# Both feed-forward products by seven quadrant products per 1024 block, inner rows and merged rows through DRAM

## The reference, cut to what matters

```python
D_MODEL, SEQ, D_FF = 1024, 1024, 4096
...
y = g[:, :, 0] * y_a + g[:, :, 1] * y_b + g[:, :, 2] * y_c
mix = y @ w_out
x = x + rmsnorm(mix, ln_mix_post)
h = rmsnorm(x, ln_mlp_pre)
x = x + rmsnorm(jnp.square(jax.nn.relu(h @ w_up)) @ w_down, ln_mlp_post)
```

## Time and profile before

| | before |
|---|---|
| median of 3 runs | 4586.25 us (4578.94 to 4586.79) |
| the profiled execution: its own time, its span | 4588.66 us, 4586.9 us |
| mean granted TensorE clock | 0.965 |
| busy share of the span: PE, DVE, ACT, POOL | 91%, 55%, 39%, 14% |
| last section (`closing`) | merge stage from about 3735 us, matmuls of the feed-forward part 3873.0 to 4576.3 us, end at 4586.9 us |

### The profile page before, as it was taken

One profiled execution on the slowest core, in us unless ns is written; L12 is line 12 of the kernel. 1 busy time (PEld: TensorE's weight loads), 2 busy tenths in 40 slices (PEclk: granted clock), 3 DMA queues, 4 the chain that ended last, 5 costly groups with the idle time before them and its releaser, 6 DMA issues. The chain is left out here.

```text
span 4586.9 us, 66646 instructions
## 1 busy us (share of the span) xinstructions
PE 4186.2 (91%) x26765; PEld 3263.0 (71%) x26765; DVE 2513.5 (55%) x3323; ACT 1799.9 (39%) x3273; POOL 657.2 (14%) x759
## 2 busy tenths in 40 slices
PE   7999889889988979999999997788589979999999
PEld 1887667668756767888887785565388855888887
DVE  1413777651277756555656553787577756334333
ACT  0312456431145642222223333777566513423222
POOL 0200400020030010000102200776212101000000
PEclk9999999999999989999999998899799989999999
DMA  7434411134331131333333232112211056323322
GB/s 268 160 112 155 143 60 49 63 135 142 117 128 55 44 129 56 119 102 103 117 101 120 101 120 78 47 62 89 95 43 39 30 200 236 110 101 129 101 92 83
DMA packets 250802, 485.61 MB, mean 106 GB/s; under 512 B 33048, under 2 KB 73208, under 8 KB 250124
## 3 DMA queue, kind: packets, MB, share of 16 engines
q1 hardware_dynamic: 250512, 481.60, 30.4%
HBM read 360.42 MB, written 121.13 MB: 105 GB/s over the span
## 5 line engine op out<-in xcount | busy, mean ns | idle before, releaser
L1028 DVE TENSOR_TENSOR p_tl<-spare,p_th 128x1024 fp32r<-128x1024 f32 x156 | 199.4, 1279 | 359.4 <-ACT p_th L900 359.4
L900 ACT CAST p_th<-spare 128x1024 fp32r<-128x1024 f32 x156 | 163.5, 1049 | 566.7 <-PE p_ps L852 566.7
L316 PE MATMUL p_ps<-p_wh,hi 128*128 128x512 f32 x896 | 352.2, 393 | 5.7 <-DVE p_wl L484 5.7
L316 PE MATMUL p_ps<-p_wh,lo 128*128 128x512 f32 x896 | 350.2, 391 | 0.0
L316 PE MATMUL p_ps<-p_wl,hi 128*128 128x512 f32 x896 | 350.1, 391 | 0.0
L852 PE MATMUL p_ps<-p_th,p_xh 128*128 128x512 f32 x784 | 310.2, 396 | 2.0 <-DVE p_tl L1028 2.0
L852 PE MATMUL p_ps<-p_th,p_xl 128*128 128x512 f32 x784 | 309.9, 395 | 0.0
L852 PE MATMUL p_ps<-p_tl,p_xh 128*128 128x512 f32 x784 | 309.9, 395 | 0.0
L852 PE MATMUL p_ps<-p_xh,p_th 128*128 128x512 f32 x672 | 263.1, 391 | 1.0 <-DVE p_tl L1028 1.0
L852 PE MATMUL p_ps<-p_xh,p_tl 128*128 128x512 f32 x672 | 263.7, 392 | 0.0
L852 PE MATMUL p_ps<-p_xl,p_th 128*128 128x512 f32 x672 | 262.6, 391 | 0.0
(11 more groups left out here) (422 smaller groups left out, 9902.8 us busy)
## 6 DMA issues: line engine op xcount, KB each, us to landing
spare<-w_in SPq DMA_DIRECT2D x56, 1024.0 KB, 5.6
p_raw<-w_in SPq DMA_DIRECT2D x40, 1024.0 KB, 5.9
pn_dram<-p_stg SPq DMA_DIRECT2D x128, 256.0 KB, 2.0
spare<-w_down SPq DMA_DIRECT2D x32, 1024.0 KB, 4.8
spare<-w_up SPq DMA_DIRECT2D x30, 1024.0 KB, 5.3
p_dram<-p_stg SPq DMA_DIRECT2D x112, 256.0 KB, 2.1
m_w<-w_mod SPq DMA_DIRECT2D x12, 2048.0 KB, 11.8
pt_dram<-p_stg SPq DMA_DIRECT2D x96, 256.0 KB, 2.2
```

The costliest lines, as they stand in the source:

```text
L316: mm = pe.matmul(ps[:, u, :], lhsT, rhs, start=(kk == 0 and q == 0), stop=(kk == KD - 1 and q == 2))
L900: act.copy(th[:, g % 2], (R11, T, R21, R12, R22, R11, R21)[i][:, 2 * u:2 * u + 2]).then_inc(s_hi, 1)
L1028: dve.tensor_tensor(tl[:, g % 2], (R11, T, R21, R12, R22, R11, R21)[i][:, 2 * u:2 * u + 2], th[:, g % 2], ALU.subtract).then_inc(s_lo, 1)
```

## The change

Both feed-forward products are now done like the projections, for all 1024 rows at once: each 1024x1024x1024 block, four for w_up and four for w_down, is seven products of 512x512x512 quadrants and sums of quadrants, 14 units of 24 matmuls (56 products of 48 matmuls, 2688 matmuls; 3072 before). A unit is still three fp32r matmuls for each tile of a pair.

- *Up block.* x, turned and normed, stands in four quadrants A11 to A22; five more of the seven operands are made of them once (S1 to S4), and all seven are split into xh and xl (128x2048 each; five of the splits stand in the queues of the first up block). The weight quadrants R11 to R22 are loaded per block, T1 to T4 are their sums on VectorE, and each unit is cast (th, ACT) and its remainder made (tl, DVE). The product tiles are joined on VectorE (`joined`), relu is on ScalarE, and the square is now on GpSimd (64 of 128x512). SP stores the result to `h_dram`.
- *Down block.* Hidden quadrants H11 to H22 come back from `h_dram`; their sums are four 128x2048 operations a block on GpSimd, in place, and both operands of every unit are split on the fly (th, tl and sh, sl). Product tiles are added into seven accumulators (`gathered`); with the last block GpSimd and VectorE combine these, ScalarE makes row sums behind waits for them (s_u2, s_c21, s_c22) that stand between its casts, and `final` adds the result to the merged rows.
- *Merge stage.* The residual rows have two buffers, xr, in place of x_sb; the merged rows go to `xm_dram` (`store_x`) and come back at the end. The load of a tile's rows waits for the store and the norm of the tile two before (s_xst, s_nx), and stands on SP ahead of the inputs of a later row tile. All eight row tiles are normed here; `turned_dram` is gone.
- *Addresses.* `sums` (160 bytes) and `ab2` stand ahead of `spare`, whose place is free in `closing`.

The diff, cut to its core:

```diff
-                    sp.wait_ge(s_y, NT)
+                if t >= 2:
+                    sp.wait_ge(s_xst[t % 2], 16 * (t // 2))
+                    sp.wait_ge(s_nx, t - 1)
+                sp.dma_start(xr[:, t % 2, :], C.x_dram[DEPTH - 1][t * P:(t + 1) * P, :]).then_inc(s_x[t % 2], 16)
+
+            def store_x(t):
+                sp.wait_ge(s_xf, t + 1)
+                sp.dma_start(xm_dram[t * P:(t + 1) * P, :], xr[:, t % 2, :]).then_inc(s_xst[t % 2], 16)
...
+                q = NQ + f
+                sp.wait_ge(s_S4, f + 1)
+                sp.wait_ge(s_hl, UN * f + 6)
+                load_hidden(f + 1, 0)
+                sp.wait_ge(s_hl, UN * f + 8)
+                load_hidden(f + 1, 3)
+                sp.wait_ge(s_lo, UN * q + 8)
+                load_block(q + 1, 2)
+                sp.wait_ge(s_hl, UN * f + 10)
+                load_hidden(f + 1, 2)
+                sp.wait_ge(s_lo, UN * q + 10)
+                load_block(q + 1, 0)
+                sp.wait_ge(s_lo, UN * q + 12)
+                load_block(q + 1, 1)
+                sp.wait_ge(s_hl, UN * f + 14)
+                load_hidden(f + 1, 1)
+                sp.wait_ge(s_lo, UN * q + 14)
+                load_block(q + 1, 3)
...
+            def triples(n, u, j, cols):
+                x = XS[n % NOPS]
+                b = (2 * n + u) % 2
...
+                    else:
+                        pairs = ((sh[:, b, k, cols], th[:, b, k, :]), (sh[:, b, k, cols], tl[:, b, k, :]), (sl[:, b, k, cols], th[:, b, k, :]))
...
+                act.copy(th[:, n % 2], source(n)).then_inc(s_hi, 1)
+                if n >= UP:
+                    v = n - UP
+                    f = v // UN
+                    ready, count = ((s_H[0], 16 * (f + 1)), (s_H[1], 16 * (f + 1)), (s_S2, f + 1), (s_H[3], 16 * (f + 1)), (s_S3, f + 1), (s_S1, f + 1), (s_S4, f + 1))[i]
+                    act.wait_ge(ready, count)
+                    act.copy(sh[:, v % 2], hidden(v)).then_inc(s_hh, 1)
...
+            for n in range(16 * NQ):
+                pool.wait_ge(s_r, n + 1)
+                x = stg[:, n % 4, :]
+                pool.tensor_tensor(x, x, x, ALU.mult).then_inc(s_q, 1)
+            for f in range(NQ):
+                pool.wait_ge(s_H[2], 16 * (f + 1))
+                pool.wait_ge(s_H[3], 16 * (f + 1))
+                if f > 0:
+                    pool.wait_ge(s_hl, UN * (f - 1) + 12)
+                else:
+                    pool.wait_ge(s_xl, 4)
+                pool.tensor_tensor(HS[:], H21[:], H22[:], ALU.add).then_inc(s_S1, 1)
+                pool.drain()
+                pool.wait_ge(s_H[0], 16 * (f + 1))
+                pool.tensor_tensor(H21[:], H11[:], H21[:], ALU.subtract).then_inc(s_S3, 1)
+                pool.drain()
+                pool.wait_ge(s_hl, UN * f + 2)
+                pool.tensor_tensor(H11[:], HS[:], H11[:], ALU.subtract).then_inc(s_S2, 1)
+                pool.drain()
+                pool.wait_ge(s_hl, UN * f + 4)
+                pool.tensor_tensor(H12[:], H12[:], H11[:], ALU.subtract).then_inc(s_S4, 1)
+            pool.wait_ge(s_C, last + 8)
+            pool.tensor_tensor(c11[:], c11[:], a1[:], ALU.add).then_inc(s_c11, 1)
+            pool.wait_ge(s_C, last + 12)
+            pool.tensor_tensor(u6[:], u6[:], a1[:], ALU.add).then_inc(s_u2, 1)
+            pool.drain()
+            pool.tensor_tensor(p3[:], p3[:], u6[:], ALU.add).then_inc(s_pre, 1)
+            pool.wait_ge(s_C, last + 16)
+            pool.tensor_tensor(p4[:], p4[:], u6[:], ALU.add).then_inc(s_pre, 1)
+            pool.wait_ge(s_fp, 16)
+            pool.wait_ge(s_sq, HT)
+            gain(c11, 0)
+            pool.wait_ge(s_C, last + 20)
+            pool.tensor_tensor(u6[:], u6[:], p7[:], ALU.add).then_inc(s_u3, 1)
+            pool.wait_ge(s_sq, 2 * HT)
+            gain(p4, 0)
...
+            def unit_lo(n):
+                if n >= ALL:
+                    return
+                dve.wait_ge(s_hi, n + 1)
+                dve.tensor_tensor(tl[:, n % 2], source(n), th[:, n % 2], ALU.subtract).then_inc(s_lo, 1)
+                if n >= UP:
+                    v = n - UP
+                    dve.wait_ge(s_hh, v + 1)
+                    dve.tensor_tensor(sl[:, v % 2], hidden(v), sh[:, v % 2], ALU.subtract).then_inc(s_hl, 1)
...
+            def T1(q):
+                for b in range(2):
+                    dve.wait_ge(s_R[b], 16 * (q + 1))
+                dve.tensor_tensor(R12, R12, R11, ALU.subtract).then_inc(s_T1, 1)
+
+            def T2(q):
+                dve.wait_ge(s_R[3], 16 * (q + 1))
+                dve.drain()
+                dve.tensor_tensor(T[:], R22, R12, ALU.subtract).then_inc(s_T2, 1)
...
+            def gathered(f, i, j):
+                n = NP + NOPS * f + i
+                dve.wait_ge(s_pm, 4 * n + j + 1)
+                to = acc[i][:, j, :]
+                if f == 0:
+                    dve.tensor_copy(to, tile(n, j)).then_inc(s_C, 1)
+                else:
+                    dve.tensor_tensor(to, to, tile(n, j), ALU.add).then_inc(s_C, 1)
...
+            def final(n, t, first, second):
+                dve.wait_ge(s_rs, n + 1)
+                j = t % HT
+                x = xrow(t)
+                dve.tensor_tensor(second[:, j, :], second[:, j, :], post[:, CH:], ALU.mult)
+                dve.scalar_tensor_tensor(x[:, 0:CH], first[:, j, :], ms[:, t, 3:4], x[:, 0:CH], ALU.mult, ALU.add)
+                dve.drain()
+                dve.scalar_tensor_tensor(x[:, CH:], second[:, j, :], ms[:, t, 3:4], x[:, CH:], ALU.mult, ALU.add).then_inc(s_fx, 1)
...
+            for n in range(ALL):
+                q, i, u = n // UN, n % UN // 2, n % 2
+                unit_lo(n + 2)
+                if n % UN == 0:
+                    T1(q)
+                elif n % UN == 1:
+                    T2(q)
+                elif n % UN == 3:
+                    T4(q)
+                elif n % UN == 5:
+                    T3(q)
...
+                    for j in range(4):
+                        gathered(f, i, j)
+                        if f == NQ - 1 and i == 6:
+                            final(j, HT + j, p4, u6)
+                    if f == NQ - 1 and i == 4:
+                        dve.wait_ge(s_pre, 2)
+                        dve.drain()
+                        for j in range(4):
+                            dve.tensor_tensor(p4[:, j, :], p4[:, j, :], p7[:, j, :], ALU.add).then_inc(s_c21, 1)
+                    if f == NQ - 1 and i == 5:
+                        dve.wait_ge(s_u3, 1)
+                        dve.drain()
+                        for j in range(4):
+                            dve.tensor_tensor(u6[:, j, :], u6[:, j, :], w5[:, j, :], ALU.add).then_inc(s_c22, 1)
+                        for j in range(4):
+                            dve.tensor_tensor(p3[:, j, :], p3[:, j, :], w5[:, j, :], ALU.add)
+                        dve.drain()
...
-        spare = sb("spare", [P, KD * D])
+        C.ab = sb("ab2", [P, NT, 2 * C_HEADS])
+        C.sums = sb("sums", [P, 8 + 4 * NT])
+        s4 = s2.enter_context(ExitStack())
+        spare = sb("spare", [P, KD * D], F32, s4)
...
```

More of the change, by code:

```diff
@@ L3208, in closing @@
         s_x = [sem(f"x_loaded{b}") for b in range(2)]
+        s_xst = [sem(f"merged_rows_stored{b}") for b in range(2)]
         s_y = sem("y_ready")
@@ L3306, in _ @@
-            for t in range(TT):
-                store(0, t)
-            for n in range(NW + 1, 2 * NW):
-                for b in range(2):
-                    weights(b, n)
-            for t in range(TT):
-                store(1, t)
+                if t == NT - 3:
+                    sp.wait_ge(s_y, NT - 1)
+                    for b in range(4):
+                        load_block(0, b)
+                if t >= 1:
+                    store_x(t - 1)
+                    if t + 1 < NT:
+                        load_x(t + 1)
@@ L3313, in _ @@
+            sp.wait_ge(s_c11, 1)
+            sp.wait_ge(s_u2, 1)
+            sp.dma_start(post, ins["ln_mlp_post_2"][0].partition_broadcast(P)).then_inc(s_fp, 16)
+            for n, t in enumerate([*range(HT, NT), *range(HT)]):
+                sp.wait_ge(s_fx, n + 1)
+                store_out(t)
             sp.wait_ge(s_out, 16 * NT)
@@ new lines, in partial, with relu @@
+            def partial(q, j):
+                act.wait_ge(s_pm, 4 * NOPS * q + j + 1)
+                if q > 0:
+                    act.wait_ge(s_C, ADDS * (q - 1) + added[5] + 2 * j + 1)
+                else:
+                    act.wait_ge(s_sum, 4)
+                act.copy(U1[:, j, :], tile(NOPS * q, j)).then_inc(s_U, 1)
+            def relu(q, i, j):
+                act.wait_ge(s_C, ADDS * q + added[i] + (2 * j if i == 5 else j) + 1)
+                act.activation(stg[:, j, :], stg[:, j, :], ACT.Relu).then_inc(s_r, 1)
@@ L3497, in _, with row_sums @@
+            def row_sums(t, half, rows):
+                act.activation(waste, rows[:, t % HT, :], ACT.Square, accum_out=ms[:, t, half:half + 1]).then_inc(s_sq, 1)
```

(51 more changed lines are left out.)

599 lines of the change are left out of this document (296 added, 303 removed).

## The result

The changed kernel takes **4627.44 us** (median of 4 runs, 4622.98 to 4632.63) against 4586.52 before, 40.9 us slower. The ratio on record is 1.0093, 95% interval 1.0075 to 1.0110 (the two medians alone give 1.0089). Forecast were 4624, a range of 4572 to 4668, and slower with a chance of 0.73.

A forecast was written before the change was run, and what follows sets the result against it. TensorE's gapless matmul stream was taken as the bound: 87.0 us saved by fewer matmuls and 5.5 of waits, against added delays, summed to +38; 4588.66 + 38 - 2.4 gave 4624 us, range 4572 to 4668.

The forecast's parts named there:

- merge stage: Stage before the feed-forward products: loads wait behind the store and norm, so y comes late; +5.5 us (0 to 14).
- before the first product: Start of the up product: last transposes wait for square, roots and scaled copy, 6.0 plus 2.0 of clock; +8 us.
- first up block; others: Up product: queued splits of x make units 6 and 8 late, +5.5 us; other up blocks +2.
- down blocks, all: Down product: +24.5 us at the first block, +36 at three boundaries, +40 in the last block.
- tail: After the last matmul: VectorE is four tiles behind, 15.4 us where 6.4 passed before; +9 us.
- The bound and the gain: Feed-forward section: a matmul stream at 0.2267 us each; 384 fewer save 87.0 us, and 5.5 of waits go.
- The lock: Down product: GpSimd's 128x2048 sums, estimated 4.5 us, stop VectorE's SBUF work for the whole instruction; 70 us hang on it.
- rival (b): Down product: GpSimd's sums fit between VectorE's instructions, or the lock binds one way; 4554 us, chance 0.15.
- The walk: Last down block, stepped through by queue: units 6, 8, 10, 12/13 late by 4.5, 8.1, 5.5, 11.8 us; clock 10.
- 3.7, and by the same steps 1.8 for the later ones: Merge stage: y late by 3.7 us from the gated load, later ones by 1.8; together +5.5 us.
- Rival (d): Merge stage, gated by stores, loses over 20 us more; chance 0.05.
- Rival (c): Second block's tiles shift by 32 modulo 64 bytes and matmul pitch worsens; up to +21 us, 4645, chance 0.12.

The follow-up runs named there:

- e1: Changed kernel with the four hidden sums of each down block shrunk on GpSimd from 512 to 8 columns a row, same waits: 4567.0 us.
- e2: Changed kernel with each hidden sum on GpSimd issued whole, but as four instructions of 128x512: 4596.1 us.
- e12: Changed kernel with the four hidden sums of each down block on VectorE, the first block's made during the last up block: 4574.7 us.
- e6: Kernel with hidden sums and last-block GpSimd operations in pieces (4597.0 us), plus c11 and c21 row sums and c21 additions one product later: 4588.4 us.
- e5: Changed kernel with four residual-row buffers instead of two in the merge stage, and stores one tile later: 4609.5 us.
- e9: All parts together (pieces, first sums early, row sums later, four row buffers; 4562.4 us), plus weight sums T1 and T2 earlier: 4551.1 us.
- e11: All parts together with T1 and T2 earlier and hidden sums on VectorE (4559.6 us), plus the last product unit by unit: 4558.3 us.

## Why the prediction was right, and where it wasn't

Terms of the sum, forecast and as the trace of the changed kernel has them (us):

| term | forecast | measured |
|---|---|---|
| 384 matmuls fewer | -87.0 | -87.0 (three up blocks at 228.7, 0.2269 a matmul) |
| old waits gone (measured: all beyond the pitch) | -5.5 | -6.8 |
| merge stage | +5.5 | **+20.0** |
| before the first product | +8 | +7.4 |
| first up block; others | +5.5; +2 | +8.0; +0.2 |
| down blocks, all | +100.5 | +90.7 |
| tail | +9 | +7.1 |
| sum | +38 | +39.6 |

The two profiles lie 34.3 us apart, since what runs ahead of the merge stage was 5.5 shorter in this one; such differences (the stage's start lies between 3739 and 3757 in the profiles here) come with any kernel and are in no term.

**The bound and the gain** were right: pitch and clock stand in the up product's windows. **The lock** was right, by rows and by e1, e2 and e12. Without sums on GpSimd (e1) the four block losses fall by 58.6 us and the time by 60.4, where the prediction had 70 hanging on the lock; rival (b), that they fit between VectorE's instructions, is out. GpSimd's estimated 4.5 was 4.6 in the rows without interference. The Trainium skill, page "SBUF — State Buffer", section "SBUF: two separate sides", has an exclusive lock for a whole instruction; the trace agrees, with 1.23 becoming 5.56 beside GpSimd and PSUM reads staying at 0.62 a tile. Inside the term the sizes were off both ways: a boundary lost 13 to 14.5 (12 forecast: the waits 4.1 + 4.7 against 8.4, the rest, which goes with the clock, some 4 to 5.5 against 3); the first down block without its share of a boundary some 21 against 24.5 (waits 11.86 and 3.93 against 12.6 and 5); and the last block with its own waits some 28 against 40. The walk had four waits there, 29.9 us, and 10 of clock; the trace has none at unit 6 where 4.5 were walked, 21.7 us in the other three, and some 6 behind them. There the hidden sums have a small part (e1 keeps 30.3), and e6, with GpSimd's work in pieces, shows that 14 of 33 us were the place of ScalarE's and VectorE's combining work in their queues, with a half of that given back in the tail.

**The merge stage** is the step that failed: "3.7, and by the same steps 1.8 for the later ones". I walked one row tile and took the next ones as nearly free. But with two buffers the load of rows waits for the norm of the tile two before, the inputs of the next tile wait behind it, and that tile's norm waits for them: the delay comes again for every pair, 8 us the first time (tile 4, counted from the first transpose of y) and 11 the next, not once. e5 shows it: with four buffers, the stores one tile later and the same bytes, 18 of the 20 us are gone. The forecast time was right partly because this error (+14.5) and those of the down blocks (-10) and the tail (-2) point opposite ways, which is luck. With this term at its measured size and no other error the sum would have been 4639, still inside the range. Rival (d) had a gate in this stage, by the stores and at over 20 us more, with 0.05; its sign, y late by more than 4 us with DMA not full, did show, but SP's long wait was for the norm (55.0 us), and for stores to land only 13.7.

**Rival (c), addresses**, is out: the changed kernel's units keep 5.44 us, and the projections run from 1803.2 to 2817.3, 1014.1 us, as they did from 1806.6 to 2820.7.

**The first up block** lost 8.0 where 5.5 were walked, by other parts: of the two late units only unit 6 shows, with a wait of 2.50; unit 8 has none. The first two units took 7.59 and 6.36 us, behind a wait of 5.35 before the last transposes and with a granted clock of 0.58 from 3894.9 to 3900.0; the walk had that clock in the term before it.

**Three slips in the working** change none of this. The cast, cast and remainder that are said to take 3.7 add up to 3.3 (the trace has 3.45 from the first one's start to the last one's end), so the slack was up to 2.1, still under half of the lock. The time of y comes to 3808.5 by its own terms, not 3809.1, so that step is 3.1, not 3.7, further from the 20 measured. And in the earlier trace rows VectorE's instruction ended 0.54 after GpSimd's, not 0.69.

What stays open: how much of the last block's 13.6 us in e9 could be had. e11 took 6.9 out of that block and the tail gave 7 back; nothing tried shortens both.

## What to carry to other kernels

Before moving elementwise work from VectorE to an idle GpSimd, price it twice: its length there (4.6 us here for what VectorE does in 2.29) is also what VectorE can lose, unless VectorE reads PSUM (0.62 a tile here beside a running sum) or idles just then. Here the busier engine doing all of it itself made the same algorithm 1.1% faster, and turned a loss into a gain. A wait in front of a DMA issue gates all that is behind it in the queue: look for the loop that it closes (load, use, norm, load), and multiply the delay by its rounds. And a wait for one engine's result that stands in a queue ahead of casts which TensorE needs sooner stops TensorE too, however idle the engine looks: with ScalarE busy for 36 of 109 us, moving such waits one product later took 14 us out of the last block (e6), though the tail gave 7 back.

## What the runs showed of the hardware that I had not expected

The profile's length of a GpSimd instruction holds its own wait for VectorE. A 128x2048 sum reads 4.6 when it starts first, also while VectorE's T2 waits for it (4.60 at 4326.43, beside the 6.74), and 5.3 to 6.3 when it starts while an instruction of VectorE runs: the sum at 4292.37 reads 5.33 because VectorE's remainder runs until 4293.29. So the two engines stop each other, each for the rest of the other's instruction. In four pieces a sum took 6.0 to 8.1 at a boundary; a piece reads 1.29 when nothing is in front of it, 2.3 behind a remainder and 3.4 behind T2. A run of short GpSimd instructions thus lengthens each of VectorE's remainders (1.23 to 2.3), where one long one stops one of them for all of its length. Waits of 4.1 and 4.7 us cost TensorE's clock as well: over the stretch of the changed kernel from 4332.9 to 4343.0, which begins with the second, the granted clock was 0.66.
